# One batch of four gate steps per attention unit, with the turns directly behind the next unit's query-key products

## The reference

```python
q, k = partial_rope(q), partial_rope(k)                  # 4 heads, 2 components of 64
s = einsum('bqhcd,bkhcd->bhcqk', qi, k) * scale           # per block of queries
s = where(chunk[None, :] <= ci[:, None], s, -inf)         # chunks of 64
p = softmax(s, axis=-1)
a = p[:, :, 0] - lam * p[:, :, 1]
o = einsum('bhqk,bkhe->bqhe', a, v)
...
gates = sigmoid(gate_logits)                              # 3 branches x 1024, from the same input
merged = sum(gates * up, axis=2)
```

## Time and profile before

| | |
|---|---|
| median of 3 runs | 2714.21 us (2710.44 to 2716.08) |
| the profiled execution's own time | 2718.18 us |
| its span | 2716.4 us |
| PE busy | 2659.3 us (98%) |
| PEld busy | 2437.0 us (90%) |
| DVE busy | 1833.6 us (68%) |
| ACT busy | 1134.1 us (42%) |
| POOL busy | 362.2 us (13%) |
| mean granted clock | 0.995 |

### The profile page before, as it was taken

The page is one execution under the profiler, slowest core; times in us unless marked ns, Lnnn a source line. Parts: engine busy times, 40 slices in busy tenths (PEclk is TensorE's granted clock), DMA queues, the critical chain, the costliest instruction groups (busy, mean ns, idle before and its releaser), DMA issues.

```text
span 2716.4 us, 55970 instructions
## 1 busy us (share of the span) xinstructions
PE 2659.3 (98%) x24543; PEld 2437.0 (90%) x24543; DVE 1833.6 (68%) x2800; ACT 1134.1 (42%) x1844; POOL 362.2 (13%) x219
## 2 busy tenths in 40 slices
PE   8999999999999999999999999999999999999998
PEld 7988998899999999988898899999987788877886
DVE  7744345556888746935345555988836998788887
ACT  6323324524333324433324534333323355466664
POOL 1211122121111000311122221111100000010001
PEclk9999999999999999999999999999999999999999
DMA  4211222264334343211222253334332322399996
GB/s 149 75 47 38 85 85 75 77 219 148 132 125 140 121 144 114 78 57 35 77 90 79 67 191 128 116 126 140 117 113 75 105 82 105 135 386 387 395 392 247
DMA packets 114204, 373.19 MB, mean 137 GB/s; under 512 B 13072, under 2 KB 14240, under 8 KB 113568
## 3 DMA queue, kind: packets, MB, share of 16 engines
q1 hardware_dynamic: 88848, 303.97, 32.9%
q10 hardware_dynamic: 18592, 41.92, 4.4%
q0 software_dynamic: 6512, 23.62, 2.3%
HBM read 336.44 MB, written 31.94 MB: 136 GB/s over the span
## 4 chain that ended last, share of the span: by engine, by line
PE 85%; DVE 9%; ACT 3%; issue 1%; DMA 1%; POOL 0%; ACTq 0%; DVEq 0%; SPq 0%; POOLq 0%
PE PS L316 83%; DVE ARENA L1214 1%; DVE ARENA L846 1%; DVE HR L482 1%; ACT ARENA L408 0%; PE PS L3279 0%; PE PS L1430 0%; DVE RINGR L311 0%; DVE ARENA L848 0%; PE PS L919 0%; DVE H L492 0%; DVE ARENA L813 0%; ACT ARENA L410 0%; DVE ARENA L815 0%; DVE WR L3268 0%
## 5 line engine op out<-in xcount | busy, mean ns | idle before, releaser
L316 PE MATMUL PS<-HR,HIGHR 128*128 128x264 f32 (+1 forms) x2976 | 845.1, 284 | 2.0 <-issue 2.0
L316 PEld LDWEIGHTS PS<-HR,HIGHR 128*128 128x128 f32 x2976 | 561.5, 189 | 2.6
L316 PE MATMUL PS<-XR,HIGHR 128*128 128x264 f32 (+2 forms) x1760 | 549.9, 312 | 5.9 <-ACT STAGE L612 5.3
L300 ACT CAST HIGHR<-RING 128x1024 fp32r<-128x1024 f32 (+2 forms) x340 | 330.6, 977 | 289.2 <-DMA RING<-wts 109.4
L316 PE MATMUL PS<-XR,RINGR 128*128 128x264 f32 (+1 forms) x1568 | 445.7, 284 | 1.6 <-issue 1.6
L316 PE MATMUL PS<-HH,HIGHR 128*128 128x264 f32 (+2 forms) x1472 | 424.5, 288 | 2.8 <-DVE RINGR L311 1.4
L316 PE MATMUL PS<-HH,RINGR 128*128 128x264 f32 (+2 forms) x1472 | 421.3, 286 | 0.0
L311 DVE TENSOR_TENSOR RINGR<-RING,HIGHR 128x1024 fp32r<-128x1024 f32 (+2 forms) x272 | 311.4, 1150 | 115.6 <-ACT HIGHR L300 115.4
L316 PEld LDWEIGHTS PS<-XR,HIGHR 128*128 128x128 f32 x1760 | 332.5, 189 | 30.2 <-issue 9.3
L316 PE MATMUL PS<-ARENA 64*64 64x64 f32 (+10 forms) x7866 | 300.0, 240 | 10.2 <-DVE ARENA L1214 2.7
L316 PEld LDWEIGHTS PS<-XR,RINGR 128*128 128x128 f32 x1568 | 296.5, 189 | 3.9 <-issue 3.9
(11 more groups left out here) (447 smaller groups left out, 5182.7 us busy)
## 6 DMA issues: line engine op xcount, KB each, us to landing
RING<-wts SPq DMA_DIRECT2D x324, 512.0 KB, 3.6
ARENA<-wmoe SPq DMA_DIRECT2D x204, 512.0 KB, 6.7
RING<-wts SPq DMA_DIRECT2D x52, 256.0 KB, 3.1
gates<-STAGE ACTq DMA_DIRECT2D x48, 264.0 KB, 4.3
ARENA<-gates ACTq DMA_DIRECT2D x48, 264.0 KB, 3.0
ys<-RING ACTq DMA_DIRECT2D x16, 512.0 KB
RING<-wts SPq DMA_DIRECT2D x16, 384.0 KB, 3.1
ys<-STAGE POOLq DMA_DIRECT2D x8, 512.0 KB, 6.1
```

The costliest lines, as they stand in the source:

```text
L300: e.copy(k.highR[:, hs, 0:n], k.ring[:, i % NRING, 0:n]).then_inc(*k.s["hi"].done(i))
L316: return e.matmul(out, lhsT, rhs, start=start, stop=stop, skip_group_check=True)
```

## The change

PE's four gate steps of a round stand in one batch instead of two batches of two, and `turned(u-1)` stands directly behind `scores(u)`. ACT makes one `fill` call per round instead of two, behind the exponentials; DVE and POOL have their numbers of calls cut to match. No instruction is added or removed, and the last round keeps its `fill(5)` and `fill(2)`.

```diff
@@ attention_pe
-    for u in range(len(UNITS) + 1):
-        if u < len(UNITS):
-            scores(u)
+    for u in range(len(UNITS)):
+        scores(u)
         if u:
-            fill(2 if u < len(UNITS) else 5)
             turned(u - 1)
-            fill(2)
+            fill(4)
             summed(u - 1)
+    fill(5)
+    turned(len(UNITS) - 1)
+    fill(2)
+    summed(len(UNITS) - 1)
     fill(4)
@@ attention_act
     for u in range(len(UNITS) + 1):
+        if u == len(UNITS):
+            fill()
         if u:
-            fill()
             turned(u - 1)
         if u < len(UNITS):
             soft(u)
@@ attention_dve
-    for u in range(len(UNITS) + 1):
+    for u in range(len(UNITS)):
+        soft(u)
         if u:
             fill()
-        if u < len(UNITS):
-            soft(u)
-        if u:
-            fill()
-    fill()
+    for u in range(3):
+        fill()
@@ attention_pool
-    for u in range(2 * len(UNITS) + 13):
+    for u in range(len(UNITS) + 14):
         fill()
```

## The result

The changed kernel takes 2724.32 us, the median of four runs (2721.96 to 2727.08); the kernel before takes 2714.78, also in four (2710.44 to 2716.08). The ratio is 1.0043 with a 95% interval of 1.0031 to 1.0055: slower, by 9.5 us between the medians. (The ratio isn't the quotient of the medians, which is 1.0035; both lie in the interval.) The forecast was 2725.9.

What follows compares the result with a forecast made beforehand. PE was taken to bound both attention loops. Terms 2 x (1.44 + 3.86 - 0.3) = 10.0 us, with the clock 11.7, set on the median 2714.2, gave 2725.9 us; range 2718 to 2731.

Steps and rivals of the forecast that it cites:

- What bounds the kernel: Both attention loops are bound by PE; moving its instructions can win back about 1.4 us in all.
- T(0), 1.44 us a layer: First transpose still starts at 392.08, waiting for DVE; twelve gate matmuls now come after it: +1.44 us per layer.
- T(1) to T(7), 3.86 less 0.3 a layer: These transposes wait for ACT's bank-emptying copy, 3.86 us per layer; cheaper borders of 16-row transposes give back 0.3.
- F: End of a round's last gate step on PE, 0.12 us behind the start of the last gate matmul.
- `AB` in time: DVE's difference is ready before PE's transposes need it; T(6) holds by 0.15 us, so no cost was taken.
- S: PE time from the end of a round's last gate step until `summed` and next `scores` are issued: 0.71 to 1.75 us.
- the 0.37 of the prediction: Forecast wait of T(4) for ACT's copy after an even round: 1.37 - 1.00 = 0.37 us.
- The clock, one fall of two: PE's 2.33 us pause before T(0), once per layer, drops the granted clock in one of two layers: +1.7 us.
- The sum: Both layers together 10.0 us, with the clock 11.7 us, set on the median 2714.2: 2725.9 us.
- Faster batches: 19 removed borders per layer at 0.09 us bring back 3.4 us in both layers: 2710.8 us; chance 0.04.
- The banks are not late: ACT's copy is ready in time, leaving T(0) and some collisions: 2719.5 us, or 2717.1 with T(0) alone; chance 0.13.
- The chains are late too: POOL and DVE collisions also hit late tiles, or the clock drops more often: 2729 to 2733 us; chance 0.13.

Runs made afterwards that it cites:

- The last version above: Kernel before the change, with fill(3) ahead of T(0) and fill(1) behind it in round 1 instead of two and two: 2711.67 us, ratio 0.9995.
- three and three steps: Changed kernel with fill(3) ahead of T(0) and fill(3) behind it in round 1: 2714.28 us, ratio 1.0005.
- the kernel that isolates it: Changed kernel with ACT's cast ahead of the tanh and its copy directly behind the tanh, T(0) uncovered: 2716.19 us, ratio 1.0022.
- the first experiment: Changed kernel with ACT's copy that empties banks 4 and 5 directly behind the tanh, ahead of DMA and cast: 2721.61 us, ratio 1.0029.
- the four kernels with T(0) uncovered: Changed kernel as is (2724.32 us), with ACT's copy moved early (2721.61), with its cast ahead of the tanh (2719.75), with both moves (2716.19).
- the two kernels of the section on the cast alone: Changed kernel with ACT's cast ahead of the tanh: 2719.75 us; the same with the copy also directly behind the tanh: 2716.19 us.
- the run with both edits: Changed kernel with ACT's copy directly behind the tanh and round 1 in the old order, fill(2) before and behind T(0): 2719.45 us, ratio 1.0027.

## Why the prediction was right, point by point

- **What bounds the kernel.** Right: PE, with about 1.4 us to win in both loops. The last version above got 1.5 us out of them, and three and three steps 1.7, once the twelve gates are taken off.
- **T(0), 1.44 us a layer.** Right: the last interval is 1.43 and 1.45 us longer, T(0) came 0.15 us after `AB` in both, and the kernel that isolates it has loops 1.4 and 1.1 us over before.
- **T(1) to T(7), 3.86 less 0.3 a layer.** The mechanism was right for T(1), T(2), T(3) and T(5), which waited for the copy in both layers. T(6) and T(7) came 0.05 us behind the copy's end too, but with no idle time to see; T(4) was released by `AB`. The size was 0.6 us too high. Without the fall of the clock the intervals from T(0) to T(8) hold 3.0 us more than before (second layer: 0.75, 0.41, 0.91, 0.43, 0.46, 0.01, 0.03, -0.01). The term that was mis-sized is the 0.15 us from the end of the copy to T(u), which I took from DVE: from ACT it was 0.05 (1434.03 + 0.18 = 1434.21 to 1434.26). With the six turns that follow the copy that is 0.6. Single turns differ by more: T(3) of the second layer waited 0.83 us and that of the first 0.54, because the tanh ahead of it started 0.55 us behind F instead of 0.25. Why it did is open.
- **`AB` in time.** I worked out T(6) and found 0.15 us of margin; it did come at the border, 0.2 us behind `AB`. I did not work out T(4), where S is 1.00 instead of 1.33. There `AB` decided in both layers: T(4) came 0.15 us behind `AB` and 0.22 and 0.28 behind the copy, where 0.05 is enough. The first layer of the changed kernel, with the shift of unit 4 held up by POOL:

```profile
404.66 2.39 POOL L311 TENSOR_TENSOR RINGR<-RING,HIGHR 128x1024 fp32r<-128x1024 f32 x1 [6.84 <-ACT HIGHR L300]
405.02 2.06 DVE L1620 TENSOR_SCALAR ARENA<-ARENA 128x2 f32<-128x2 f32 x1
...
408.70 0.37 DVE L1631 SCALAR_TENSOR_TENSOR ARENA<-ARENA 128x144 f32<-128x144 f32 x1
...
409.22 0.27 PE L1430 MATMUL PS<-CST,ARENA 128*16 128x128 f32 x1 [0.21 <-DVE ARENA L1631]
```

  That the interval ahead of T(4) grew by 0.4 us, as the 0.37 of the prediction has it, is luck: the wait was another one. "I take nothing" for `AB` was off by those 0.2 us only, but hid how close it was: without the late copy it costs up to 1.1 us a unit (T(4) and T(6) of the first experiment, first layer; 0.65 and 0.3 for T(8) and T(10)).
- **The clock, one fall of two.** The profiled execution had exactly one, at 1.3 us instead of 1.7, since the end of the slow stretch fell into the time in which PE waited for the copy anyway (T(1) then waited 0.82 us instead of 1.03). Over the four kernels with T(0) uncovered it was four falls of eight, at up to 1.5 us. One of two is borne out on average; that this execution had just one is chance, as the two kernels of the section on the cast alone had two and none. The prediction also lets the rule that it cites from the Trainium skill bring a fall after every pause. The rule as cited says which rate is the default and not which pauses lead to it, so it doesn't by itself give two falls.
- **The sum.** 10.0 without the clock was 8.7 (4.2 or so in the first layer, 4.4 in the second); with it 11.7 was 10.0 in the loops, and 9.5 in the medians. The interval of the ratio, 1.0031 to 1.0055, is 8.4 to 14.9 us, so the times alone confirm the sum no more closely than that; the loops do.
- **The rivals.** Faster batches: refuted by the run with the new order in the late rounds. "The banks are not late": refuted by the trace of the changed kernel. "The chains are late too": in this kernel at T(4) only, 0.2 us, but it is what two of the experiments ran into.

## What to carry to other kernels

When work that covers a chain is moved behind it, every chain that it covered must be followed, not only the longest: here the turn's input, the copy that frees its banks, and an unrelated cast that stood in ACT's order ahead of that copy. A wait can hide another that is a little shorter, so taking away the one that the profile names may give back little (here 0.5 of some 6 us); look for the instruction that feeds both, here the cast, and move it into its own engine's idle time. Before making batches larger to save borders, measure one border: here 128-row operands cost nothing at it, and the 1.4 us of idle PE in the loops was the most that covering waits could have won.

## What was not expected of the hardware

- A pause of PE of 2.25 us was followed by a fall of the granted clock to 0.50 in four of eight cases with nearly the same program around it; each cost 1.3 to 1.5 us. In the changed kernel the fall came at 391.0, 1.6 us after the pause had ended at 389.37; in the kernel with the early copy it came as the pause ended. A shorter pause was followed by one too, the 1.72 us ahead of T(1) in the run with both edits, while the 1.60 us of the earlier trace rows was not. What decides between the cases wasn't tried.
- Where PE waited, it followed ACT's copy 0.05 us after its end, and DVE's difference 0.15 us after its end (389.00 + 0.22 = 389.22 to 389.37 in the changed kernel).
- The phase of a batch against the bank's four steps alone, with no work moved between engines, took the waits for the copy and for `AB` out of the loop, but for the 0.1 us at two 16-row units.
